# A two-block forward pass in fp32: the low parts of six of 434 chunks of weights are computed by GpSimd in place of VectorE

## The chip, the core and the metric

The kernel runs on one NeuronCore of one Trainium2 chip, as one program. The metric is the device time of one execution, in microseconds (us). Before the change it is 2494.46 us, the median of three runs between 2493.82 and 2494.64. The engines are named TensorE (PE in the rows), VectorE (DVE), ScalarE (ACT), GpSimd (POOL) and SyncE (SP).

## The reference, cut to what matters

256 tokens of width 2048 go through two blocks, each a mixer and an MLP around a residual stream. All is fp32, and nearly all of the time goes to products with weights.

```python
def first_block(x, ...):                     # one layer
    h = x + gla_mixer(rmsnorm(x, gla_norm), gla_w_in, ..., gla_w_out)
    h = h + sq_relu_mlp(rmsnorm(h, mlp_norm), mlp_w_up, mlp_w_down)
    return rmsnorm(h, final_norm)

def hybrid_mixer(xn, w_in, ...):             # the second block's mixer
    proj = xn @ w_in
    dn_qkv, dn_z, dn_a, dn_b, swa_q, swa_kv, sb_qkv, gates = split_cols(proj, IN_SIZES)
    dn_qkv = silu(causal_dwconv(dn_qkv, dn_conv))
    q, k, v = split_cols(dn_qkv, ...)        # 8 heads of 128
    q, k = l2norm(q), l2norm(k)
    o_dn = gated_delta_rule(q, k, v, g, beta)   # chunks of tokens; a triangular solve in each
    ...
    return merged @ w_o

def second_block(x, mem, ...):
    h = x + hybrid_mixer(rmsnorm(x, norm_mix), ...)
    h = h + memory_cross_attention(rmsnorm(h, norm_xattn), rmsnorm(mem, norm_mem), ...)
    h = h + conv_ffn(rmsnorm(h, norm_ffn), w_up, ffn_conv, w_down)
    return rmsnorm(h, norm_final)
```

The part that the change touches is `xn @ w_in` of the second block (its columns for queries, keys, values and z of the delta rule) and, beside it, the norms of q and k and the solve of the delta rule.

## The kernel before, in words

**Weights as a stream.** All weights lie in memory as 434 chunks of 128 x 2048 fp32 (1 MB), in the order in which they are used. TensorE takes them in a format of less precision (fp32r), so each chunk is split: ScalarE copies it, rounded, into `w_hi` (the high part, line 1044), and VectorE subtracts this from the raw chunk to get `w_lo` (the low part, line 1677). The activations are split likewise into `x_hi` and `x_lo`. A chunk is four tiles of 128 x 512; for each tile and each half of the tokens `chunk` (from line 508) issues three matmuls of 512 columns: high by high (L528), high by low (L529), low by high (L530). That makes 24 matmuls per chunk.

**Slots.** There are four slots. `w_raw` and `w_lo` share memory, so the subtraction works in place. SyncE loads chunk c when TensorE has finished chunk c - 4 (semaphore `used`). ScalarE and VectorE split the chunk that lies three ahead (`AHEAD = 3`) of the one for which they do their other work; their programs are written out by hand, step c of each holding the side work of chunk c and then `split(c + 3)`. TensorE waits ahead of chunk c for the semaphore `lo_ready` to have counted that far.

**The stretch.** The second block begins with chunk 192, and its chunks are counted here from there: chunk 18 is 192 + 18. Chunks 0 to 23 are queries, keys and values of the delta rule, 24 to 31 are z. Beside them, TensorE does side work between chunks, in this order from chunk 18 on:

- after 18: `nN` of the keys (products that turn them into rows, L693), then the products `kk` (L684); after 19: the products `qk` (L684); after 20: the transposes `dT` of the values (L548);
- after 24: `vN` of the first half of the values (L693) and the last `dT` (L548); after 26: the first products of the solve (L745); in the middle of 27: `vN` of the last half (L693), which waits for the semaphore `conv_out`, 6, that is for VectorE's `cv<-th,cv` (L1974) of step 25.

**VectorE's side work.** Step 19: the sum of squares `ssk` of the keys (L1978, L1983), `qkT`, `xT_c`, `xn_c`. Step 20: three taps of the convolution (L1965) and the scales from `rk`. Step 21: `cv<-th,cv` (L1974) and the opening of the solve, `xn_c` (L2022, L2023), `xT_c` (L2026), `xTb_c` (L2027), `am_c` (L2044). Steps 22 and 23: `am_c` and splits. Step 25: L1974 again.

**GpSimd** does small work: powers of minus one half for the norms (L461, L481, L483, L488), a memset of `xT` (L479), and issues some DMAs. `rk`, the inverse norms of the keys, is such a power of `ssk` (128x16, semaphore `ss_ready`, 2).

Of the kernel before, what the change touches and what calls it, by code (L numbers as in the profile page):

```python
# [16 lines left out]
def build(nc, x, x_turned, mem, mem_turned, stream, cols, rows, wglow, wab, wgu, shapes, masks, out):  # L17
# [14 lines left out]
    F32, F32R, BF16 = mybir.dt.float32, mybir.dt.float32r, mybir.dt.bfloat16  # L32
    ACT, ALU, AX = mybir.ActivationFunctionType, mybir.AluOpType, mybir.AxisListType
    N = 512
    NB = D // N
    SLOTS = 4
    AHEAD = 3
    EARLY = 4
    NCHUNK = stream.shape[0]
# [4 lines left out]
    with ExitStack() as ctx:  # L44
        def sem(name):
            return ctx.enter_context(nc.semaphore(name))
# [9 lines left out]
        def sb(name, shape, dt=F32, offset=None):  # L56
            nbytes = (2 if dt == BF16 else 4) * int(np.prod(shape[1:]))
            return nc.alloc_sbuf_tensor_at(name, shape, dt, offset=take(nbytes) if offset is None else offset)
# [4 lines left out]
        w_raw = sb("w_raw", [P, SLOTS, CH], F32, a_raw)  # L63
        w_lo = sb("w_lo", [P, SLOTS, CH], F32R, a_raw)
        w_hi = sb("w_hi", [P, SLOTS, CH], F32R)
# [158 lines left out]
        hi_ready, lo_ready, used = sem("hi_ready"), sem("lo_ready"), sem("used")  # L224
        tp_done = sem("tp_done")
        took = {k: {e: [sem(f"{k}_took_{e}{p}") for p in range(2)] for e in ("act", "dve")} for k in ("acc", "tp")}
        cols_in, cst_in, mask_in, gla_in, row_in, out_done = [sem(s) for s in ("cols_in", "cst_in", "mask_in", "gla_in", "row_in", "out_done")]
        x_in = sem("x_in")
        w_part = [[sem(f"w_part{c}_{k}") for k in range(4)] for c in range(EARLY)]
        gain_in, xT_in, x0_high, x0_low = sem("gain_in"), [sem(f"xT_in{n}") for n in range(NB + 1)], sem("x0_high"), sem("x0_low")  # L230
# [88 lines left out]
        ROUNDED = {name: k for k, name in enumerate(name for name in SIDE if name not in ("sbq", "sbk", "xk"))}  # L319
        LAST = {("norm1", 3): 1, ("merged", 3): 2, ("norm6", 3): 3}  # L320

        def ready(c, k=3):
            return 4 * c + k + 1 if c < EARLY else 3 * EARLY + c + 1

        def landing(c):
            return 16 * (c // SLOTS + (1 if c % SLOTS >= EARLY else 0))
# [71 lines left out]
        C_GLA, C_OUT, C_MLP, C_2 = 0, 48, 64, 192  # L398
# [47 lines left out]
        @block.gpsimd  # L446
        def _(pool):
            pool.memset(mhalf[:], -0.5).then_inc(pool_set, 1)
            pool.memset(glow[:], 0.0).then_inc(pool_set, 1)
            pool.wait_ge(w_part[2][3], 16)  # L450
            pool.dma_start(col[:, 16:N_COLS], cols[:, 16:N_COLS]).then_inc(cols_in, 16)
            pool.dma_start(wg_raw[:], wglow).then_inc(wg_in, 16)
            for r in range(4):
                pool.dma_start(w_gu[32 * r:32 * r + 16], wgu).then_inc(gla_in, 16)
            pool.dma_start(onorm[:], rows[:, 0:N]).then_inc(gla_in, 16)
            pool.wait_ge(pool_set, 1)
            mh8 = mhalf[:].rearrange("p (m h) -> p m h", m=M)

            def norm(j, count, k=0):
                pool.wait_ge(var_ready[k], count)  # L460
                pool.tensor_tensor(rstd[:, j], var[k][:], mhalf[:, 0:M], ALU.pow).then_inc(rstd_ready[k], 1)  # L461

            norm(0, 1)
            for hd in range(4):
                pool.wait_ge(ovar_s, hd + 1)
                pool.tensor_tensor(orstd[:, hd], ovar[:, hd], mhalf[:, 0:M], ALU.pow).then_inc(orstd_s, 1)

            pool.wait_ge(b_turned, SIDE["y", 3] + 1)
            pool.dma_start(frow[:], rows[:, N:N + D]).then_inc(row_in, 16)
            pool.dma_start(tri_c[:], shapes[:, 3 * P + SEQ:4 * P + SEQ]).then_inc(dn_in, 16)  # L470
            pool.dma_start(wab_raw[:], wab).then_inc(dn_in, 16)
            pool.dma_start(tri[:], shapes[:, 2 * P + SEQ:3 * P + SEQ]).then_inc(smalls_in, 16)
            pool.dma_start(lvl[:], masks[:, 0:6 * 32]).then_inc(smalls_in, 16)
            pool.dma_start(row_p[:], rows[:, N + 2 * D:]).then_inc(smalls_in, 16)
            norm(1, 2)

            norm(2, 3)
            norm(3, 4)
            pool.memset(xT[:], 0.0).then_inc(pool_set, 1)  # L479
            pool.wait_ge(ss_ready, 1)  # L480
            pool.tensor_tensor(rq[:], ssq[:], mh8, ALU.pow).then_inc(r_pow, 1)  # L481
            pool.wait_ge(ss_ready, 2)
            pool.tensor_tensor(rk[:], ssk[:], mh8, ALU.pow).then_inc(r_pow, 1)  # L483

            pool.wait_ge(tp_done, tps.name["up"] + 1)
            pool.dma_start(amask[:], masks[:, 6 * 32:]).then_inc(amask_in, 16)
            pool.wait_ge(y_var, 1)
            pool.tensor_tensor(yrs[:], yss[:], mh8, ALU.pow).then_inc(y_pow, 1)  # L488

            pool.wait_ge(used, C_WO)  # L490
            pool.dma_start(m_raw[:], mem_turned).then_inc(memT_in, 16)
            pool.wait_ge(b_low, ROUNDED["merged", 3] + 1)
            pool.dma_start(memt[:], mem.rearrange("(m p) n -> p m n", p=P)).then_inc(mem_in, 16)
            norm(4, 1, 1)
            norm(5, 5)

            pool.wait_ge(sq_done[1], 8)
            pool.dma_start(cw_all[:], cols[:, N_COLS:]).then_inc(cw_in, 16)
            norm(6, 6)
            pool.dma_start(frow2[:], rows[:, N + D:N + 2 * D]).then_inc(row2_in, 16)  # L500
            for m in range(M):
                pool.wait_ge(fin_var, m + 1)
                pool.tensor_tensor(rstd[:, 7, m:m + 1], var[1][:, m:m + 1], mhalf[:, 0:1], ALU.pow).then_inc(fin_rstd, 1)
# [3 lines left out]
        def _(pe):  # L507
            def chunk(c, lhs, k0, blk, first, last, n_k=4, width=N, rows_=(0, 1), done=True, second_half=None):

                if c >= EARLY:  # L510
                    pe.wait_ge(lo_ready, ready(c))
                if first and blk >= 2:

                    accs.wait(pe, blk - 2)
                wh = w_hi[:, c % SLOTS].rearrange("p (k n) -> p k n", n=width)
                wl = w_lo[:, c % SLOTS].rearrange("p (k n) -> p k n", n=width)
                for k in range(n_k):
                    if second_half and k == n_k // 2:
                        second_half()
                    if c < EARLY:  # L520
                        pe.wait_ge(lo_ready, ready(c, k))
                    if c < NB:
                        pe.wait_ge(x0_low, 4 * c + k + 1)
                    for m in rows_:
                        xh = lhs[0][:, k0 + k, m * P:(m + 1) * P]
                        xl = lhs[1][:, k0 + k, m * P:(m + 1) * P]
                        dst = acc[:, blk % 2, m, 0:width]
                        pe.matmul(dst, xh, wh[:, k], start=first and k == 0, stop=False)  # L528
                        pe.matmul(dst, xh, wl[:, k], start=False, stop=False)  # L529
                        mm = pe.matmul(dst, xl, wh[:, k], start=False, stop=last and k == n_k - 1)  # L530
                if done:
                    mm.then_inc(used, 1)
                return mm
# [108 lines left out]
            for c in range(48):  # L642
                b, q = divmod(c, 4)
                chunk(C_GLA + c, X, 4 * q, accs.name[("gla", b)], q == 0, q == 3)
                if c == 3:
                    pe.wait_ge(wg_l, 1)
                    sixteen_columns("glow_rows", wg)
                if c == 6:
                    pe.wait_ge(cst_in, 16)
                    sixteen_rows_back("glow", "glow_rows", glow_rows)  # L650
                if c == 8:
                    low_rank_transposed()
                if c == 10:
                    gate_logits()
                gla_side(c)

            for c in range(16):
                b, q = LATER(4)[c]
                if b == 0:
                    pe.wait_ge(b_low, ROUNDED["y", q] + 1)  # L660
                chunk(C_OUT + c, A, 4 * q, accs.name[("glaout", b)], q == 0, q == 3)
                gla_side(48 + c)
# [264 lines left out]
            for nb in range(NB):  # L927
                for j in range(16):
                    c = 50 + 16 * nb + j
# [734 lines left out]
        def _(dve):  # L1664
# [7 lines left out]

            def split(c):

                if c < NCHUNK:
                    dve.wait_ge(hi_ready, ready(c))
                    dve.tensor_tensor(w_lo[:, c % SLOTS], w_raw[:, c % SLOTS], w_hi[:, c % SLOTS].bitcast(F32),  # L1677
                                      ALU.subtract).then_inc(lo_ready, 1)
# [161 lines left out]
            for c in range(64):  # L1840
# [41 lines left out]
                if c and c not in (8, 10, 20, 24):  # L1882
                    split(c + AHEAD)
# [333 lines left out]
            for nb in range(NB):  # L2217
                for j in range(16):
                    c = 50 + 16 * nb + j
# [305 lines left out]
```

## Time and profile before

| what | value |
|---|---|
| median of the runs | 2494.46 us |
| the profiled execution, its time | 2494.04 us |
| its span, first to last instruction | 2492.2 us |
| mean granted TensorE clock (share of full) | 0.999 |
| TensorE busy | 2481.5 us, 100% |
| VectorE busy | 1490.1 us, 60% |
| ScalarE busy | 1541.5 us, 62% |
| GpSimd busy | 33.4 us, 1% |
| low parts on VectorE (L1677) | 430 of them, 983.6 us |

Busy time of TensorE is counted from the start of a matmul to its modelled end, and matmuls overlap, so 100% doesn't mean its peak. Idle time of the other engines costs nothing by itself. Times of rows are from the span's start.

### The profile page before, as it was taken

Reading aid. Unit: us, or ns where it says so; the run is one execution under the profiler, and the core shown is the slowest. Engines: PE = TensorE matmul, PEld = TensorE weight load, DVE = VectorE, ACT = ScalarE, POOL = GpSimd, SP = SyncE. Lnnn points to the kernel's source line nnn. Section 1 sums busy time; section 2 is a strip of 40 time slices with the busy share of each in tenths; the row PEclk is TensorE's granted clock in tenths of the full one; section 3 lists DMA queues with packets and bytes.
Section 4 is the critical chain, followed back from the end, with each engine's and each line's share of the span. In section 5 each row is a group of like instructions: output and inputs, shape, how many; then the busy total and the mean of one; then the engine's idle time right before and its main releaser. Section 6 shows DMA issues by size and latency. Waiting matters only on the chain.

```text
span 2492.2 us, 29745 instructions
## 1 busy us (share of the span) xinstructions
PE 2481.5 (100%) x12494; PEld 2051.3 (82%) x12494; DVE 1490.1 (60%) x1223; ACT 1541.5 (62%) x2041; POOL 33.4 (1%) x41
## 2 busy tenths in 40 slices
PE   9999999999999999999999999999999999999998
PEld 7887788888888888888888888888888888888887
DVE  5775656545545545666765665545565677646675
ACT  6645777636537547766465565535587688638873
POOL 0000000000000000000000000000000000000000
PEclk9999999999999999999999999999999999999999
DMA  8554555555555555545444445555655555555554
GB/s 287 187 200 163 187 200 187 199 188 196 192 193 196 190 199 187 201 169 187 154 160 145 155 162 193 193 196 189 267 188 185 186 188 199 187 198 191 195 193 152
DMA packets 69366, 472.37 MB, mean 190 GB/s; under 512 B 7912, under 2 KB 8352, under 8 KB 13424
## 3 DMA queue, kind: packets, MB, share of 16 engines
q1 hardware_dynamic: 67040, 460.62, 51.6%
q0 software_dynamic: 1312, 7.73, 0.8%
q8 instruction: 98, 1.61, 0.3%
q10 hardware_dynamic: 880, 2.11, 0.2%
q14 instruction: 36, 0.29, 0.0%
HBM read 468.33 MB, written 2.11 MB: 189 GB/s over the span
## 4 chain that ended last, share of the span: by engine, by line
PE 98%; DVE 1%; ACT 1%; issue 1%; DMA 0%; SPq 0%; POOLq 0%; POOL 0%; DVEq 0%; ACTq 0%
PE acc L528 31%; PE acc L530 31%; PE acc L529 31%; PE tp L812 1%; PE tp L548 0%; PE tp L745 0%; DMA x_raw<-in_x_turned 0%; PE tp L684 0%; PE tp L693 0%; DVE cv L1965 0%; DVE w_lo L1677 0%; PE tp L563 0%; PE tp L564 0%; PE tp L612 0%; PE tp L960 0%
## 5 line engine op out<-in xcount | busy, mean ns | idle before, releaser
L1677 DVE TENSOR_TENSOR w_lo<-w_raw,w_hi 128x2048 fp32r<-128x2048 f32 x430 | 983.6, 2289 | 730.9 <-ACT w_hi L1044 729.0
L1044 ACT ACTIVATE w_hi<-w_raw 128x2048 fp32r<-128x2048 f32 x430 | 823.0, 1916 | 482.4 <-DMA w_raw<-in_stream 462.3
L528 PE MATMUL acc<-w_hi,x_hi 128*128 128x512 f32 (+1 forms) x2240 | 875.1, 391 | 0.7 <-DVE w_lo L1684 0.4
L530 PE MATMUL acc<-w_hi,x_lo 128*128 128x512 f32 (+1 forms) x2240 | 868.4, 388 | 0.0
L529 PE MATMUL acc<-w_lo,x_hi 128*128 128x512 f32 (+1 forms) x2240 | 868.3, 388 | 0.0
L528 PEld LDWEIGHTS acc<-w_hi,x_hi 128*128 128x128 f32 x2240 | 420.6, 188 | 89.6 <-issue 2.0
L530 PEld LDWEIGHTS acc<-w_hi,x_lo 128*128 128x128 f32 x2240 | 420.6, 188 | 86.6
L529 PEld LDWEIGHTS acc<-w_lo,x_hi 128*128 128x128 f32 x2240 | 420.7, 188 | 85.5 <-issue 1.0
L528 PE MATMUL acc<-w_hi,a_hi 128*128 128x512 f32 x1120 | 436.3, 390 | 0.1
L530 PE MATMUL acc<-w_hi,a_lo 128*128 128x512 f32 x1120 | 435.7, 389 | 0.0
L529 PE MATMUL acc<-w_lo,a_hi 128*128 128x512 f32 x1120 | 435.7, 389 | 0.0
L528 PEld LDWEIGHTS acc<-w_hi,a_hi 128*128 128x128 f32 x1120 | 210.2, 188 | 43.9 <-DVE a_lo L2314 0.5
L530 PEld LDWEIGHTS acc<-w_hi,a_lo 128*128 128x128 f32 x1120 | 210.2, 188 | 43.7
L529 PEld LDWEIGHTS acc<-w_lo,a_hi 128*128 128x128 f32 x1120 | 210.2, 188 | 43.5
L1061 ACT ACTIVATE nat<-acc,rstd 128x512 f32<-128x512 f32 (+1 forms) x96 | 60.2, 679 | 115.2 <-PE acc L530 114.8
L1590 ACT ACTIVATE fm<-fturned 32x256 f32<-32x256 f32 x256 | 106.2, 415 | 4.2 <-DVE fturned L2355 1.2
L1244 ACT ACTIVATE sq<-turned 32x256 f32<-32x256 f32 x256 | 106.0, 414 | 3.0
L1753 DVE TENSOR_TENSOR h<-acc,h 128x1024 f32<-128x1024 f32 x35 | 42.8, 1223 | 43.9 <-PE acc L530 43.9
L1061 ACT ACTIVATE nat<-acc,rhalf 128x512 f32<-128x512 f32 x36 | 22.8, 686 | 72.2 <-PE acc L530 72.2
L1083 ACT ACTIVATE sq<-turned 32x256 f32<-32x256 f32 x104 | 43.2, 416 | 11.7 <-DVE turned L1720 10.5
L528 PE MATMUL acc<-w_hi,m_hi 128*128 128x512 f32 x128 | 49.8, 389 | 0.0
L529 PE MATMUL acc<-w_lo,m_hi 128*128 128x512 f32 x128 | 49.8, 389 | 0.0
(383 smaller groups left out, 1301.3 us busy)
## 6 DMA issues: line engine op xcount, KB each, us to landing
w_raw<-in_stream SPq DMA_DIRECT2D x430, 1024.0 KB, 4.8
w_raw<-in_stream SPq DMA_DIRECT2D x16, 256.0 KB, 8.1
h<-in_x SPq DMA_DIRECT2D x4, 512.0 KB, 14.0
frow<-in_rows POOLq DMA_DIRECT2D x2, 1024.0 KB, 6.2
m_raw<-in_mem_turned POOLq DMA_DIRECT2D x1, 2048.0 KB, 10.2
memt<-in_mem POOLq DMA_DIRECT2D x1, 2048.0 KB, 8.9
x_raw<-in_x_turned SPq DMA_DIRECT2D x3, 512.0 KB, 8.3
dec<-gc_rows ACTq DMA_DIRECT2D x1, 1024.0 KB, 6.1
```

What stands on the lines that cost most here:

```text
L528: pe.matmul(dst, xh, wh[:, k], start=first and k == 0, stop=False)
L529: pe.matmul(dst, xh, wl[:, k], start=False, stop=False)
L530: mm = pe.matmul(dst, xl, wh[:, k], start=False, stop=last and k == n_k - 1)
L812: mm = pe.matmul(tpf(g)[:, hd * P:(hd + 1) * P], lhs(hd), rhs(hd), start=True, stop=True)
L1044: act.activation(w_hi[:, c % SLOTS], w_raw[:, c % SLOTS], ACT.Copy).then_inc(hi_ready, 1)
L1061: ins = act.activation(dst[:, m], src[:, m], func, scale=scales[:, j, m:m + 1])
L1083: ins = act.activation(dst[32 * to:32 * to + 32, :, :, q], src[32 * q:32 * q + 32, :, :, to], ACT.Copy)
L1244: ins = act.activation(dst[32 * to:32 * to + 32, :, :, q], src[32 * q:32 * q + 32, :, :, to], ACT.Square)
L1590: ins = act.activation(dst[32 * to:32 * to + 32, :, :, q], src[32 * q:32 * q + 32, :, :, to], ACT.Copy)
L1677: dve.tensor_tensor(w_lo[:, c % SLOTS], w_raw[:, c % SLOTS], w_hi[:, c % SLOTS].bitcast(F32), ALU.subtract).then_inc(lo_ready, 1)
L1753: dve.tensor_tensor(hn, acc[:, blk % 2], hn, ALU.add).then_inc(accs.sem(blk), 1)
```

## The change

A list `POOLED` names six chunks, 18, 20, 22, 24, 26 and 28 of the second block. VectorE's `split` leaves them out. GpSimd's program gets a `split` of its own, with the same subtraction, which waits for the same high part and counts a semaphore of its own, `lo_pooled`. TensorE waits for `lo_pooled` ahead of a pooled chunk, and for `lo_ready`, less the pooled chunks so far, ahead of any other. GpSimd executes its row in order: the subtraction of chunk 18 stands between the powers for `rq` and `rk`, that of chunk 20 behind the power for `rk`.

```diff
+        POOLED = [192 + c for c in range(18, 30, 2)]
+
         def ready(c, k=3):
             return 4 * c + k + 1 if c < EARLY else 3 * EARLY + c + 1
+
+        def low_ready(eng, c):
+            if c in POOLED:
+                eng.wait_ge(lo_pooled, POOLED.index(c) + 1)
+            else:
+                eng.wait_ge(lo_ready, ready(c) - sum(1 for p in POOLED if p < c))
...
             pool.wait_ge(ss_ready, 1)
             pool.tensor_tensor(rq[:], ssq[:], mh8, ALU.pow).then_inc(r_pow, 1)
-            pool.wait_ge(ss_ready, 2)
-            pool.tensor_tensor(rk[:], ssk[:], mh8, ALU.pow).then_inc(r_pow, 1)
+            def split(c):
+                pool.wait_ge(hi_ready, ready(c))
+                pool.tensor_tensor(w_lo[:, c % SLOTS], w_raw[:, c % SLOTS], w_hi[:, c % SLOTS].bitcast(F32), ALU.subtract).then_inc(lo_pooled, 1)
+
+            for c in POOLED:
+                if c == C_2 + 20:
+                    pool.wait_ge(ss_ready, 2)
+                    pool.tensor_tensor(rk[:], ssk[:], mh8, ALU.pow).then_inc(r_pow, 1)
+                split(c)
...
                 if c >= EARLY:
-                    pe.wait_ge(lo_ready, ready(c))
+                    low_ready(pe, c)
...
             def split(c):
 
-                if c < NCHUNK:
+                if c < NCHUNK and c not in POOLED:
                     dve.wait_ge(hi_ready, ready(c))
```

Below, each row is one instruction: its line, its operation, out<-in by the program's names, the shape, and the semaphores it waits for. GpSimd's row around the powers, before:

```order
L479 MEMSET xT 128x2048
L481 TENSOR_TENSOR rq<-ssq,mhalf 128x16 [waits ss_ready]
L483 TENSOR_TENSOR rk<-ssk,mhalf 128x16 [waits ss_ready]
L486 DMA amask<-in_masks 128x768 [waits tp_done]
L488 TENSOR_TENSOR yrs<-yss,mhalf 128x16 [waits y_var]
```

and with the change (lines are those of the changed kernel, 8 to 15 further down):

```order
L487 MEMSET xT 128x2048
L489 TENSOR_TENSOR rq<-ssq,mhalf 128x16 [waits ss_ready]
L492 TENSOR_TENSOR w_lo<-w_raw,w_hi 128x2048 [waits hi_ready]
L497 TENSOR_TENSOR rk<-ssk,mhalf 128x16 [waits ss_ready]
L492 TENSOR_TENSOR w_lo<-w_raw,w_hi 128x2048 [waits hi_ready] x5
L501 DMA amask<-in_masks 128x768 [waits tp_done]
L503 TENSOR_TENSOR yrs<-yss,mhalf 128x16 [waits y_var]
```

One subtraction (chunk 18) stands ahead of the power for `rk`, five behind it, of which the first is chunk 20's.

VectorE's row from the low part of chunk 23 on (its first row here), before; the second low part is chunk 24's, the two in one row those of 25 and 26:

```order
L1677 TENSOR_TENSOR w_lo<-w_raw,w_hi 128x2048 [waits hi_ready,dve_step]
L1974 SCALAR_TENSOR_TENSOR cv<-th,cv 128x1024 [waits conv_t]
L2022 TENSOR_TENSOR xn_c<-xn_c,b_123 128x512
L2023 TENSOR_TENSOR xn_c<-lvl,xn_c 128x512 [waits dve_step]
L2026 STREAM_TRANSPOSE xT_c<-xn_c 128x512 [waits x_first]
L2027 TENSOR_TENSOR xTb_c<-xT_c,b_123 128x512 [waits dve_step]
L2044 TENSOR_TENSOR am_c_151<-aT_c,lvl 128x512 [waits dve_step]
L1677 TENSOR_TENSOR w_lo<-w_raw,w_hi 128x2048 [waits hi_ready]
L2044 TENSOR_TENSOR am_c_150<-aT_c,lvl 128x512
L1677 TENSOR_TENSOR w_lo<-w_raw,w_hi 128x2048 [waits hi_ready] x2
L1965 SCALAR_TENSOR_TENSOR cv<-tp,col,cv 128x255 [waits conv0]
```

and with the change:

```order
L1692 TENSOR_TENSOR w_lo<-w_raw,w_hi 128x2048 [waits hi_ready,dve_step]
L1989 SCALAR_TENSOR_TENSOR cv<-th,cv 128x1024 [waits conv_t]
L2037 TENSOR_TENSOR xn_c<-xn_c,b_123 128x512
L2038 TENSOR_TENSOR xn_c<-lvl,xn_c 128x512 [waits dve_step]
L2041 STREAM_TRANSPOSE xT_c<-xn_c 128x512 [waits x_first]
L2042 TENSOR_TENSOR xTb_c<-xT_c,b_123 128x512 [waits dve_step]
L2059 TENSOR_TENSOR am_c_151<-aT_c,lvl 128x512 [waits dve_step]
L2059 TENSOR_TENSOR am_c_150<-aT_c,lvl 128x512
L1692 TENSOR_TENSOR w_lo<-w_raw,w_hi 128x2048 [waits hi_ready]
L1980 SCALAR_TENSOR_TENSOR cv<-tp,col,cv 128x255 [waits conv0]
```

The low parts of 24 and 26 are gone, that of 25 stands directly behind the two `am_c`. Nothing else in VectorE's row changes place.

## Rows read from the trace of the kernel before

**Rows 1.** The page, busy times and costliest groups: busy us, mean ns, idle before.

```profile
PE 2481.5 (100%) x12494; PEld 2051.3 (82%) x12494; DVE 1490.1 (60%) x1223; ACT 1541.5 (62%) x2041; POOL 33.4 (1%) x41
...
L1677 DVE TENSOR_TENSOR w_lo<-w_raw,w_hi 128x2048 fp32r<-128x2048 f32 x430 | 983.6, 2289 | 730.9 <-ACT w_hi L1044 729.0
```

**Rows 2.** Timeline, TensorE: start us, us, instruction, count, idle before and its releaser.

```profile
1.19 6.15 PE L641 MATMUL acc<-junk 128*128 128x512 bf16 x16 [1.19 <-DVE junk L1807]
6.99 0.58 PE L528 MATMUL acc<-w_hi,x_hi 128*128 128x512 f32 x1
...
1188.36 0.39 PE L528 MATMUL acc<-w_hi,x_hi 128*128 128x512 f32 x1
...
1204.36 3.73 PE L684 MATMUL tp<-cqT,ckT 128*128 128x128 f32 x32
1207.84 0.48 PE L528 MATMUL acc<-w_hi,x_hi 128*128 128x512 f32 x1
...
1230.14 0.39 PE L529 MATMUL acc<-w_lo,x_hi 128*128 128x512 f32 x1
1230.37 0.39 PE L530 MATMUL acc<-w_hi,x_lo 128*128 128x512 f32 x1
1231.05 0.50 PE L528 MATMUL acc<-w_hi,x_hi 128*128 128x512 f32 x1 [0.30 <-DVE w_lo L1677]
...
1238.30 0.48 PE L528 MATMUL acc<-w_hi,x_hi 128*128 128x512 f32 x1
...
1253.45 1.03 PE L693 MATMUL tp<-consts,cv 128*128 128x128 f32 x8
...
2483.97 0.39 PE L530 MATMUL acc<-w_hi,a_lo 128*128 128x512 f32 x1
```

**Rows 3.** Timeline, GpSimd, from the memset to the power for rk.

```profile
1096.69 1.83 POOL L479 MEMSET xT<- 128x2048 f32 x1
1159.04 4.87 POOL L481 TENSOR_TENSOR rq<-ssq,mhalf 128x16 f32<-128x16 f32 x1 [60.52 <-DVE ssq L1983]
1204.12 2.90 POOL L483 TENSOR_TENSOR rk<-ssk,mhalf 128x16 f32<-128x16 f32 x1 [40.20 <-DVE ssk L1983]
```

**Rows 4.** Timeline, VectorE, around the same times and from step 19 to step 25.

```profile
1096.99 1.56 DVE L1699 TENSOR_SCALAR rhalf<-rstd 128x2 f32<-128x2 f32 x1
...
1158.87 2.29 DVE L1677 TENSOR_TENSOR w_lo<-w_raw,w_hi 128x2048 fp32r<-128x2048 f32 x1
...
1203.86 0.17 DVE L1983 TENSOR_SCALAR ssk<-ssk 128x16 f32<-128x16 f32 x1
...
1224.05 1.22 DVE L1974 SCALAR_TENSOR_TENSOR cv<-th,cv 128x1024 f32<-128x1024 f32 x1
1225.19 0.68 DVE L2022 TENSOR_TENSOR xn_c<-xn_c,b 128x512 f32<-128x512 f32 x1
...
1228.71 2.28 DVE L1677 TENSOR_TENSOR w_lo<-w_raw,w_hi 128x2048 fp32r<-128x2048 f32 x1
...
1231.52 2.28 DVE L1677 TENSOR_TENSOR w_lo<-w_raw,w_hi 128x2048 fp32r<-128x2048 f32 x1
...
1248.53 1.22 DVE L1974 SCALAR_TENSOR_TENSOR cv<-th,cv 128x1024 f32<-128x1024 f32 x1
```

**Rows 5.** Timeline, ScalarE, the high parts of chunks 18, 24 and 26.

```profile
1178.00 1.92 ACT L1044 ACTIVATE w_hi<-w_raw 128x2048 fp32r<-128x2048 f32 x1
...
1222.14 1.90 ACT L1044 ACTIVATE w_hi<-w_raw 128x2048 fp32r<-128x2048 f32 x1
...
1232.01 1.92 ACT L1044 ACTIVATE w_hi<-w_raw 128x2048 fp32r<-128x2048 f32 x1
```

**Rows 6.** Tile rhalf: duration ns min/median/max, first and last start us.

```profile
L1699 DVE TENSOR_SCALAR rhalf<-rstd x6: 169/169/1560, 52.4 to 1978.9; 128x2 f32<-128x2 f32 x6
```

**Rows 7.** Windows at the end: busy PE, PEld, DVE, ACT, POOL, granted clock, DMA.

```profile
2487.00:2488.00 1.00, 0.00 (x0) 0.00 (x0) 0.97 (x3) 0.48 (x1) 0.00 (x0) 0.91 0.00 0
2488.00:2489.00 1.00, 0.00 (x0) 0.00 (x0) 0.00 (x0) 0.00 (x0) 0.00 (x0) 0.50 0.96 348
```

More of the change, by code:

```diff
@@ L226, in build @@
         took = {k: {e: [sem(f"{k}_took_{e}{p}") for p in range(2)] for e in ("act", "dve")} for k in ("acc", "tp")}
-        cols_in, cst_in, mask_in, gla_in, row_in, out_done = [sem(s) for s in ("cols_in", "cst_in", "mask_in", "gla_in", "row_in", "out_done")]
+        cols_in, cst_in, mask_in, gla_in, row_in, out_done, lo_pooled = [sem(s) for s in ("cols_in", "cst_in", "mask_in", "gla_in", "row_in", "out_done", "lo_pooled")]
         x_in = sem("x_in")
```

## The prediction

> **What bounds the kernel now.** I read the page first: busy times, then the costliest groups. TensorE is busy for the whole span and VectorE for 60% of it [rows 1], so an edit that takes work from VectorE pays only where TensorE waits for VectorE. Then I followed TensorE in order of time through the stretch, chunks 18 to 28 of the delta rule's part (counted from its first chunk, as below). Chunk 24 is the one place where it waits for a low part: the last matmul of chunk 23 starts at 1230.37, 0.23 us behind the one before, and chunk 24 starts at 1231.05, at the end of VectorE's low part, not at 1230.60 [rows 2]. That is 0.45 us, all that six relieved chunks can give. A pitch of 0.227 us also makes a chunk's 24 matmuls 5.4 us. Next I read when each pooled chunk's high part is ready, when TensorE wants the chunk, and what GpSimd has ahead of it.
>
> **What goes, what comes.** VectorE loses six subtractions of 2.29 us [rows 1], 13.7 us of busy time. All but the last 0.45 us lies beside TensorE's work. GpSimd gains six subtractions of the same shape, in one row with its two powers, and the order shows the point on which the sum rests: the power for rk stands ahead of the low part of chunk 20 and waits for VectorE's sum ssk. Before, no chunk depended on that.
>
> **The duration of a GpSimd subtraction, X.** No row shows one. Below lies VectorE's own 2.29 us [rows 1], or still lower GpSimd's memset of the same 128x2048 at 1.83 us, which only writes [rows 3]. 1.83 us for 2048 elements is about 0.85 us per thousand for one stream after 0.1 us of start. Two reads in turn with the write beside them would take 3.6 us, two reads and the write all in turn 5.3 us. I take 4.4, the middle of these two, and keep 2.3 and 5.3 as ends. A far end is the power, 2.90 us for 16 elements [rows 3], which would make 0.37 ms of one chunk; the memset shows that moving an element doesn't cost that, and I give it no chance of weight. The Trainium skill, GPSIMD Engine Reference, section Elementwise — side-by-side cycle accounting, states 4497 ns for a two-input fp32 operation of 2048 elements; by it the sum below would be 4.1 in place of 3.9 us, and no run here shows it yet.
>
> **Chunk 18.** Its high part ends at 1178.00 + 1.92 = 1179.9 [rows 5], GpSimd is idle, and TensorE wants it at 1188.36 [rows 2]: 8.4 us of room. Cost nothing up to X = 8.4.
>
> **Chunk 20, the main term.** ssk ends at 1203.86 + 0.17 = 1204.03 [rows 4]. It isn't earlier for the two subtractions that VectorE no longer does, since products of TensorE and squares of ScalarE come before it. The power runs from 1204.12 to 1207.02 [rows 3], and the subtraction can only start then: it ends at 1207.02 + 4.4 = 1211.42. A semaphore takes 0.06 us to TensorE (1228.71 + 2.28 = 1230.99, and chunk 24 starts at 1231.05) [rows 2, 4]. So chunk 20 starts at 1211.48 in place of 1207.84 [rows 2]: a stall of **3.64 us**, called S = X - 0.76. Behind it on TensorE everything is queued, and nothing of it is won back, for TensorE has no other idle time. Chunk 22 is two chunks (10.9 us) later and GpSimd free at 1211.4, so its subtraction hides.
>
> **Chunk 24, the gain.** From here all times are of the profile before, with S to be added. High part 24 is ready at 1222.14 + 1.90 = 1224.04 [rows 5] and VectorE's low part 23 ends where cv starts, 1224.05 [rows 4]. GpSimd starts then, or behind the cv (1.2 us), and ends at 1228.5 to 1229.7, before 1230.60. The 0.45 us goes: **-0.45**.
>
> **The shared read.** Does GpSimd's subtraction hold up VectorE? The trace shows both directions. The power for rq starts at 1159.04 while VectorE's subtraction runs from 1158.87 to 1161.16, and takes 4.87 us; the same power for rk, with no such neighbour, takes 2.90 [rows 3, 4]. 1161.16 + 2.75 is its end: it stood still until VectorE had done. And a scaling of two elements on VectorE, 0.17 us in all other places, takes 1.56 us at 1096.99, until GpSimd's memset (1096.69 to 1098.52) ends [rows 3, 4, 6]. So I take it that VectorE's operations with two SBUF inputs and GpSimd's subtractions exclude each other for their whole length. The Trainium skill, SBUF — State Buffer, section Who interferes with whom, states this as an exclusive lock, taken by whoever issues first, for two-input VectorE operations against GpSimd's reads: by that rule, the trace agrees with its 4.87 against 2.90 us. Without such a lock the sum would be 3.64 - 0.45 = 3.2 us, and the first rival below would not exist.
>
> **Who is held up.** (a) Chunk 28: low part 27 ends on VectorE at about 1248.53, where cv starts [rows 4]; GpSimd, waiting, gets its turn and holds it until 1252.93. The cv on th (1.2 us) ends at 1254.13 in place of 1249.75, and TensorE wants it in the middle of chunk 27, at 1253.45 (L693) [rows 2, 4]: a stall of 1254.13 + 0.06 - 1253.45 = **0.74 us**, the cover of 3.7 us being gone. It is nothing for X under 3.6. (b) Chunk 25: the chain xn_c to am_c starts on VectorE when both GpSimd's low part 24 and cv are through, 1224.1 + 4.4 + 1.15 = 1229.65 in place of 1225.19, 4.46 us late. Low part 25 stood at 1231.52; less the 2.2 us of low part 24 and plus 4.46 it starts at 1233.8 [rows 4]. GpSimd asks for chunk 26 when the high part is through, 1232.01 + 1.92 = 1233.93 [rows 5], and 0.09 later as after ssk: 1234.0. VectorE is first by 0.2 us, and its low part 25 is ready at 1236.1, before the 1237.85 at which it is wanted (1238.30 less the 0.45). GpSimd then works on 26 until 1240.5, wanted at 1243.3. No cost, but by 0.2 us only.
>
> **Sum.** 3.64 - 0.45 + 0.74 = 3.93 us on the profiled execution, 2494.04 us (span 2492.2). The median of the runs stands 0.42 us above it, 2494.46, and gets the same shift: **2498.4 us**, +0.16%. A measurement of this kernel tells about 0.2% (5.0 us) from no change, so this is one that would hardly be told.
>
> **Rivals.**
> 1. GpSimd takes its turn for chunk 26 ahead of VectorE's low part 25 (the slower side). It decides from X = 4.6, or 0.2 us of lost time at the hand-overs. Then GpSimd runs 1234.0 to 1238.4, low part 25 ends at 1240.7, and chunk 25, wanted at 1237.85, stalls 2.89 us; the 0.74 of chunk 27 is covered by it. 3.64 - 0.45 + 2.89 = 6.1 us: 2500.5; at X = 5.3 it is 4.54 - 0.45 + 3.79 = 7.9: 2502.3. For it: the margin is thin. Against: at 4.4 the order comes out the other way. 27%.
> 2. The stall costs the clock too. TensorE idles from the end of the products at 1204.36 + 3.73 = 1208.09 to 1211.48, 3.4 us; nowhere else does it idle so long but at the end, where its last matmul ends at 2484.36 and the granted clock is 0.91 in 2487 to 2488, and 0.50 after, which puts its fall to the lower level, 1.2 GHz, at about 2487.8, 3.5 us later [rows 2, 7]. Price: at the opening 16 matmuls of 512 columns take 5.80 us in place of 16 x 0.227 = 3.6 [rows 2, 7], so +2.2: 2500.6. 9%.
> 3. GpSimd is quicker than I take it, or excludes nothing: X = 2.3 gives 1.54 - 0.45 = 1.1 us (2495.6), X = 3.6 gives 2.4 (2496.9), no lock 3.2. 16%.
> 4. No late chunk 20 at all, the gain alone: -0.45, 2494.0. It needs X under 0.76 us, less than half of the memset. 2%, and a gain over 0.2% is nowhere to be had.
> 5. The change does something else than it says: the order shows six subtractions in GpSimd's row and six gone from VectorE's, and TensorE waits for them. 1% at most, in the rest.
>
> **Chances and range.** The forecast has 42%, its own range 2497.6 to 2499.2. The rest, 4%, is a heavier mixture, rivals 1 and 2 together. The cases from 2495.6 to 2502.0 leave out less than 2 in 10 and take in X from 2.3 to about 5.2. Slower by over 0.2% (above 2499.45) are rivals 1 and 2, the heavier mixture, and a sliver of the forecast: 41%. Faster by over 0.2%: 1%. The rest, 58%, within.
>
> **What would show it.** GpSimd's row at 1207.0 gives X, and TensorE's wait of about 3.6 us ahead of chunk 20, released by GpSimd, is the main term. Chunk 24 should start without a wait. The cv on th ahead of the middle of chunk 27 should be drawn out and TensorE wait 0.8 us for it. If TensorE waits nearly 3 us at chunk 25, rival 1 holds; matmuls at twice the pitch behind chunk 20's wait are rival 2. Wrong outright would be: no wait at chunk 20, so that the power for rk came earlier, or a long wait at chunk 18 or 22.

## The result, and the profile after

The changed kernel takes 2500.38 us, the median of 15 runs (2498.22 to 2501.90), against 2494.58 us of 15 runs before (2493.82 to 2496.05). The ratio is 1.0022, with a 95% interval of 1.0014 to 1.0030: slower by 5.8 us. The time is inside the range on record, 2 us above the forecast, and above the 2499.45 us that the prediction set as the border of slower by over 0.2%, the side to which it gave 41%. The changed kernel's runs also lie further apart, 3.7 us against 2.2.

The page of the changed kernel, busy times and the group of VectorE's low parts, which answer to [rows 1]; lines of the code are 8 to 15 further down now:

```profile
PE 2482.4 (99%) x12494; PEld 2052.3 (82%) x12494; DVE 1487.1 (60%) x1217; ACT 1540.9 (62%) x2041; POOL 64.4 (3%) x47
...
L1692 DVE TENSOR_TENSOR w_lo<-w_raw,w_hi 128x2048 fp32r<-128x2048 f32 x424 | 969.9, 2289 | 731.0 <-ACT w_hi L1059 728.8
```

VectorE has given up 13.7 us in this group but only 3 us of its busy time: other operations of it have grown longer. The view of waits, TensorE alone (us in total, times, longest), shows what is new:

```profile
PE acc L543 <- POOL w_lo L492: 3.5, 1, 3.5
PE acc L543 <- DVE w_lo L1699: 2.2, 3, 0.9
...
PE tp L708 <- DVE cv L1989: 0.6, 1, 0.6
```

The first is the wait for GpSimd at chunk 20, the last the one in the middle of chunk 27. The second lies in the opening, ahead of the change, where the first weights landed later in this execution. Everything behind it stands later: GpSimd's first power by 0.64 us (52.32 against 51.68), the products ahead of chunk 20 by 1.13 (1205.49 against 1204.36). The other 0.5 us came up before 220 us, ahead of the change too; its cause isn't known. GpSimd's timeline, which answers to [rows 3]:

```profile
1181.13 4.59 POOL L492 TENSOR_TENSOR w_lo<-w_raw,w_hi 128x2048 fp32r<-128x2048 f32 x1 [16.09 <-ACT w_hi L1059]
1205.26 2.90 POOL L497 TENSOR_TENSOR rk<-ssk,mhalf 128x16 f32<-128x16 f32 x1 [19.53 <-DVE ssk L1998]
1208.12 9.49 POOL L492 TENSOR_TENSOR w_lo<-w_raw,w_hi 128x2048 fp32r<-128x2048 f32 x2
1230.40 5.62 POOL L492 TENSOR_TENSOR w_lo<-w_raw,w_hi 128x2048 fp32r<-128x2048 f32 x1 [12.79 <-ACT w_hi L1059]
1240.21 6.54 POOL L492 TENSOR_TENSOR w_lo<-w_raw,w_hi 128x2048 fp32r<-128x2048 f32 x1 [4.19 <-ACT w_hi L1059]
1253.88 4.80 POOL L492 TENSOR_TENSOR w_lo<-w_raw,w_hi 128x2048 fp32r<-128x2048 f32 x1 [7.13 <-ACT w_hi L1059]
```

The low part of chunk 20 begins at the end of the power, as forecast. The spans of 5.62 and 6.54 us are subtractions that stand still first, until VectorE's operation of that moment is done. TensorE's timeline, answering to [rows 2]:

```profile
1205.49 3.73 PE L699 MATMUL tp<-cqT,ckT 128*128 128x128 f32 x32
1212.68 0.80 PE L543 MATMUL acc<-w_hi,x_hi 128*128 128x512 f32 x1 [3.46 <-POOL w_lo L492]
1213.28 0.63 PE L544 MATMUL acc<-w_lo,x_hi 128*128 128x512 f32 x1
...
1214.98 0.63 PE L545 MATMUL acc<-w_hi,x_lo 128*128 128x512 f32 x1
1215.41 0.47 PE L543 MATMUL acc<-w_hi,x_hi 128*128 128x512 f32 x1
...
1236.58 0.39 PE L545 MATMUL acc<-w_hi,x_lo 128*128 128x512 f32 x1
1236.81 0.39 PE L543 MATMUL acc<-w_hi,x_hi 128*128 128x512 f32 x1
...
1243.91 0.48 PE L543 MATMUL acc<-w_hi,x_hi 128*128 128x512 f32 x1
...
1259.82 1.09 PE L708 MATMUL tp<-consts,cv 128*128 128x128 f32 x8 [0.60 <-DVE cv L1989]
```

Chunk 20 starts at 1212.68, 7.19 us behind the start of the products before it, in place of 3.48. The second matmul starts 0.60 us behind the first; from there to the seventh they are 0.43 us apart and last 0.63, where the later ones are 0.23 apart and last 0.39. Chunk 24 (1236.81) follows chunk 23 without a gap. The windows of this stretch (busy PE, PEld, DVE, ACT, POOL, granted clock, DMA) say what the wide spacing is:

```profile
1211.00:1212.00 1.00, 0.00 (x0) 0.00 (x0) 1.00 (x1) 0.00 (x0) 1.00 (x1) 1.00 0.00 0
1212.00:1213.00 1.00, 0.32 (x1) 0.32 (x2) 1.00 (x1) 0.00 (x0) 1.00 (x2) 0.58 0.00 0
1213.00:1214.00 1.00, 1.00 (x3) 0.81 (x3) 0.89 (x2) 0.00 (x0) 1.00 (x1) 0.50 0.00 0
...
1215.00:1216.00 1.00, 1.00 (x5) 0.81 (x4) 0.00 (x0) 0.00 (x0) 1.00 (x1) 0.72 0.00 0
```

The granted clock fell to 1.2 GHz (0.50) while TensorE waited and came back at about 1215.6. VectorE's timeline, answering to [rows 4]:

```profile
1209.26 1.23 DVE L1946 TENSOR_TENSOR qkT<-tp,dec 128x1024 f32<-128x1024 f32 x1 [0.56 <-PE tp L699]
1210.52 2.65 DVE L2026 TENSOR_TENSOR xT_c<-aT_c,lvl 128x512 f32<-128x512 f32 x1
...
1230.33 1.22 DVE L1989 SCALAR_TENSOR_TENSOR cv<-th,cv 128x1024 f32<-128x1024 f32 x1
1231.47 5.11 DVE L2037 TENSOR_TENSOR xn_c<-xn_c,b 128x512 f32<-128x512 f32 x1
...
1240.02 2.28 DVE L1692 TENSOR_TENSOR w_lo<-w_raw,w_hi 128x2048 fp32r<-128x2048 f32 x1
...
1254.15 5.61 DVE L1989 SCALAR_TENSOR_TENSOR cv<-th,cv 128x1024 f32<-128x1024 f32 x1
```

Three operations with two SBUF inputs that took 0.7 to 1.2 us before take 2.65, 5.11 and 5.61 us: each ends where GpSimd's subtraction has ended and its own time has passed, within 0.15 us (GpSimd ends at 1236.02 and `xn_c`, 0.68 us alone, at 1236.58). `qkT`, with one input in PSUM, keeps its 1.23 us beside the same subtraction. At 1240.02 the low part of chunk 25 begins, 0.19 us ahead of GpSimd's request at 1240.21.

The parts, from these rows against [rows 2] (differences of starts, so the 1.13 us from ahead of the change drop out):

| part | forecast | in the profiled execution |
|---|---|---|
| chunk 20 late: 7.19 - 3.48 | +3.64 | +3.71 |
| clock, and the wait at chunk 24: (1243.91 - 1212.68) - (1238.30 - 1207.84) | -0.45 | +0.77 |
| middle of chunk 27: (1259.82 - 1243.91) - (1253.45 - 1238.30) | +0.74 | +0.76 |
| sum | +3.93 | +5.24 |

The span grew by 6.5 us: these 5.24, the 1.13 from ahead of the change, and 0.1 elsewhere. The middle line is two things: the gain at chunk 24 and about 1.3 us of clock (the experiment with filled idling, below, gives -0.55 for the gain alone).

### The profile page after: what moved, and what is told of

Same layout as the page of the kernel before. It is cut to its first block, busy times and chain, and to the rows that moved or that the text cites. A ratio compares the mean times of both kernels' runs of the same rounds, so it can differ in the third digit from the quotient of the medians.

```text
span 2498.7 us, 29745 instructions
## 1 busy us (share of the span) xinstructions
PE 2482.4 (99%) x12494; PEld 2052.3 (82%) x12494; DVE 1487.1 (60%) x1217; ACT 1540.9 (62%) x2041; POOL 64.4 (3%) x47
## 4 chain that ended last, share of the span: by engine, by line
PE 97%; DVE 1%; ACT 1%; issue 0%; POOL 0%; DMA 0%; SPq 0%; POOLq 0%; DVEq 0%; ACTq 0%
PE acc L543 31%; PE acc L544 31%; PE acc L545 31%; PE tp L827 1%; PE tp L563 0%; PE tp L760 0%; DMA x_raw<-in_x_turned 0%; PE tp L708 0%; DVE cv L1989 0%; DVE cv L1980 0%; DVE w_lo L1692 0%; POOL w_lo L492 0%; PE tp L578 0%; PE tp L579 0%; PE tp L627 0%
## 5 line engine op out<-in xcount | busy, mean ns | idle before, releaser
L1692 DVE TENSOR_TENSOR w_lo<-w_raw,w_hi 128x2048 fp32r<-128x2048 f32 x424 | 969.9, 2289 | 731.0 <-ACT w_hi L1059 728.8
```

## The experiments

Theory: the late power ahead of chunk 20 is the main term, a second one is VectorE held up by GpSimd's reads ahead of the middle of chunk 27, and the 2 us on top with the spread are the clock, which falls because TensorE idles. Rivals: contention makes the loss wherever the power stands; or the surplus comes from the turn for chunk 26, which the forecast had only 0.2 us from going wrong. All medians stand beside runs of the kernel before on the same chip: 2494.55 us for `rk_behind`, `only_20`, `idle_filled` and `rk_behind_no28`, 2494.46 for `half_20`, `am_twice` and `memset_28`.

**The power behind the low part of chunk 20** (`rk_behind`).

```diff
-                if c == C_2 + 20:
+                if c == C_2 + 22:
                     pool.wait_ge(ss_ready, 2)
                     pool.tensor_tensor(rk[:], ssk[:], mh8, ALU.pow).then_inc(r_pow, 1)
                 split(c)
```

> All six subtractions on GpSimd, but the power for rk stands behind the low part of chunk 20 in GpSimd's row. Theory (the late power is the main term, and the idle of TensorE it makes costs clock on top): no wait at chunk 20, granted clock full all through the stretch; the wait ahead of chunk 24 gone (-0.6 us), 0.8 us in the middle of chunk 27 stays: +0.2 us on before, 2494.8, runs as close together as before's. Rival (GpSimd's subtractions cost by holding up VectorE, wherever the power stands): still over +3 us.

Measured: 2494.79 us (2494.39 to 2495.73), ratio 1.0002 (0.9993 to 1.0011). TensorE's waits and GpSimd's timeline in it:

```profile
PE tp L708 <- DVE cv L1989: 0.6, 1, 0.6
PE acc L543 <- DVE w_lo L1699: 0.4, 1, 0.4
```

```profile
1193.01 4.77 POOL L492 TENSOR_TENSOR w_lo<-w_raw,w_hi 128x2048 fp32r<-128x2048 f32 x1 [8.18 <-ACT w_hi L1059]
1204.36 2.90 POOL L497 TENSOR_TENSOR rk<-ssk,mhalf 128x16 f32<-128x16 f32 x1 [6.58 <-DVE ssk L1998]
```

The low part of chunk 20 is through at 1197.78, 6.6 us before the power can start. The wait for GpSimd is gone, the one for cv is still there, and 5.6 of the 5.8 us have gone with one number in the code. All six subtractions still run on GpSimd, so contention wherever the power stands is not what makes the loss; what it costs is the wait of 0.6 us that is left.

**Chunk 20 alone** (`only_20`).

```diff
-        POOLED = [192 + c for c in range(18, 30, 2)]
+        POOLED = [212]
```

> Only chunk 20 is pooled, behind the power for rk. Theory: the wait of 3.7 us at chunk 20 and 0 to 3 us of lower clock behind it; chunk 24 waits for VectorE as before or a little less, nothing at chunk 27: +5 to +6 us in the median, 2500, with a spread over several us. Rival (the contention of the other five makes half of the loss): about +3.7 us and no spread.

Measured: 2499.58 us (2498.11 to 2501.16), ratio 1.0020 (1.0011 to 1.0029). TensorE's timeline and windows:

```profile
1204.69 3.73 PE L699 MATMUL tp<-cqT,ckT 128*128 128x128 f32 x32
1211.86 0.80 PE L543 MATMUL acc<-w_hi,x_hi 128*128 128x512 f32 x1 [3.44 <-POOL w_lo L492]
...
1217.58 0.51 PE L544 MATMUL acc<-w_lo,x_hi 128*128 128x512 f32 x1
...
1220.20 1.03 PE L563 MATMUL tp<-consts,nat 128*128 128x128 f32 x8
```

```profile
1210.00:1211.00 1.00, 0.00 (x0) 0.00 (x0) 1.00 (x1) 0.00 (x0) 1.00 (x1) 0.99 0.00 0
1211.00:1212.00 1.00, 0.14 (x1) 0.14 (x1) 1.00 (x1) 0.00 (x0) 0.81 (x1) 0.50 0.00 0
...
1217.00:1218.00 1.00, 1.00 (x4) 0.77 (x4) 0.00 (x0) 0.00 (x0) 0.00 (x0) 0.59 0.00 0
```

One chunk makes 5.0 of the 5.8 us and nearly the whole spread, a little below the 2500 expected. Three of the 11 runs are at 2498.11 to 2498.40, where the wait alone would put them (2494.55 + 3.7), the others at 2499.42 or above. Here the lower clock lasted from 1211.0 to 1217.8, and the chunk takes 8.34 us (1211.86 to 1220.20).

**The idling filled** (`idle_filled`).

```diff
+                if c == 212:
+                    accs.wait(pe, blk - 2)
+                    for _ in range(16):
+                        pe.matmul(acc[:, blk % 2, 0, :], junk[:, 0:P], junk[:], start=True, stop=True)
                 if c >= EARLY:
                     low_ready(pe, c)
```

> The changed kernel with 16 matmuls of 512 columns on scratch data ahead of TensorE's wait for chunk 20; they fill the 3.5 us of idling and compute nothing that is used. Theory (the clock falls because TensorE idles): chunk 20 starts at the same moment as in the changed kernel, but its matmuls are 0.23 us apart from the start: 2498.3 to 2498.6, +3.8 to +4.1 us on before, spread under 1 us. Rival (the 2 us above the forecast and the spread come from the turn for chunk 26, which TensorE would feel at chunk 25): 2500.4 and the spread of the changed kernel.

Measured: 2498.45 us (2498.14 to 2499.28), ratio 1.0016 (1.0007 to 1.0025). TensorE's timeline and one window (15 of the 16 matmuls on scratch data are in the trace):

```profile
1204.77 3.73 PE L703 MATMUL tp<-cqT,ckT 128*128 128x128 f32 x32
1208.55 3.40 PE L528 MATMUL acc<-junk 128*128 128x512 bf16 x15
1211.96 0.50 PE L547 MATMUL acc<-w_hi,x_hi 128*128 128x512 f32 x1
...
1217.55 1.03 PE L567 MATMUL tp<-consts,nat 128*128 128x128 f32 x8
...
1241.87 0.48 PE L547 MATMUL acc<-w_hi,x_hi 128*128 128x512 f32 x1
```

```profile
1212.00:1213.00 1.00, 1.00 (x5) 0.82 (x6) 0.96 (x2) 0.00 (x0) 1.00 (x1) 1.00 0.00 0
```

Chunk 20 starts 7.19 us behind the products, as in the changed kernel, but at the full clock: it takes 5.59 us (1211.96 to 1217.55) in place of 6.92 there. The median is 3.9 us above before, which is the forecast's sum, and the spread of 3.7 us has shrunk to 1.1. So the surplus over the forecast, 2500.38 - 2498.45 = 1.9 us in the median and 3.5 at most, is the clock, and it fell because TensorE idled: the two kernels differ only in the scratch matmuls. From chunk 20 to 25 it is 29.91 us against 30.46 before: the gain at chunk 24 is 0.55 us.

**Half of chunk 20** (`half_20`).

```diff
+                own = slice(CH // 2, CH) if c == 212 else slice(0, CH)
-                pool.tensor_tensor(w_lo[:, c % SLOTS], ...
+                pool.tensor_tensor(w_lo[:, c % SLOTS, own], ...
...
-                if c < NCHUNK and c not in POOLED:
+                if c < NCHUNK and (c not in POOLED or c == 212):
+                    own = slice(0, CH // 2) if c == 212 else slice(0, CH)
```

The cut also leaves out TensorE's side: ahead of chunk 20 it waits for both halves.

> The changed kernel, but of chunk 20 GpSimd takes only the second 1024 columns, behind the power for rk; VectorE takes the first 1024 in its old place. Theory (the wait is the rest of GpSimd's subtraction behind the power, and the clock falls only after a longer idling): the subtraction takes about 2.3 us in place of 4.5, TensorE waits 1.5 us at chunk 20, idles 1.3, the clock stays up: 1.5 - 0.6 + 0.8 = +1.7 us, 2496.3, no spread. Rival (any wait of that kind costs clock, or the duration of a GpSimd subtraction is mostly start-up): +3 us or more.

Measured: 2496.28 us (2495.95 to 2496.60), ratio 1.0007 (0.9998 to 1.0016). TensorE's timeline:

```profile
1204.63 3.73 PE L700 MATMUL tp<-cqT,ckT 128*128 128x128 f32 x32
1209.64 0.50 PE L544 MATMUL acc<-w_hi,x_hi 128*128 128x512 f32 x1 [1.28 <-POOL w_lo L493]
```

The wait follows the size of the subtraction (5.01 us behind the products, 1.53 more than before), and after 1.3 us of idling the clock is still full: chunk 20 takes 5.58 us (1209.64 to 1215.22), and the 11 runs lie within 0.7 us.

**One operation more ahead of the low part of chunk 25** (`am_twice`), on top of the moved power.

```diff
+                        if l == 2:
+                            link(dve.tensor_tensor(mat4(am_c[l % 2][:]), mat4(aT_c[:]), lvl[:, l + 1]..., ALU.mult))
                         dve.tensor_tensor(mat4(am_c[l % 2][:]), mat4(aT_c[:]), lvl[:, l + 1]..., ALU.mult).then_inc(m_ready, 1)
```

> The power for rk stands behind the low part of chunk 20, and VectorE does one of its am_c of step 22 twice (0.7 us more, ahead of the low part of chunk 25). Theory (turns at the shared read are taken in the order of asking, and VectorE had it for chunk 25 by 0.2 us only): GpSimd takes its turn for chunk 26 first, the low part of chunk 25 is 4.5 us late, TensorE waits about 3.6 us at chunk 25 and not at 27: +2.8 us on the kernel without the doubled operation, 2497.6, and up to 3 us more where the clock falls in that wait. Rival (GpSimd and VectorE only slow each other a little, and VectorE has 4 us of slack): 2494.8, no wait at chunk 25.

Measured: 2499.40 us (2497.43 to 2500.97), ratio 1.0020 (1.0011 to 1.0028). VectorE, GpSimd, TensorE, and two windows:

```profile
1234.47 0.69 DVE L2061 TENSOR_TENSOR am_c<-aT_c,lvl 128x512 f32<-128x512 f32 x1
1235.08 6.64 DVE L1692 TENSOR_TENSOR w_lo<-w_raw,w_hi 128x2048 fp32r<-128x2048 f32 x1
```

```profile
1234.56 5.01 POOL L492 TENSOR_TENSOR w_lo<-w_raw,w_hi 128x2048 fp32r<-128x2048 f32 x1 [4.20 <-ACT w_hi L1059]
```

```profile
1237.47 1.04 PE L563 MATMUL tp<-consts,nat 128*128 128x128 f32 x8
1241.77 0.79 PE L543 MATMUL acc<-w_hi,x_hi 128*128 128x512 f32 x1 [3.27 <-DVE w_lo L1692]
1242.36 0.63 PE L544 MATMUL acc<-w_lo,x_hi 128*128 128x512 f32 x1
```

```profile
1240.00:1241.00 1.00, 0.00 (x0) 0.00 (x0) 1.00 (x1) 1.00 (x2) 0.00 (x0) 0.97 0.85 360
1241.00:1242.00 1.00, 0.23 (x1) 0.23 (x2) 1.00 (x2) 0.99 (x1) 0.00 (x0) 0.50 0.01 0
```

GpSimd asked at 1234.56 and got its turn at about 1235.1, VectorE's subtraction of 2.3 us took 6.64, TensorE waited 3.3 us for it, and the clock fell again, at about 1240.9. This is the prediction's first rival, made to happen: 0.7 us of work on an engine with time to spare costs 4.7 us: 4.9 over its kernel before, where `rk_behind` stands 0.2 over its own. In the changed kernel's profile it didn't happen, and 1.1 us of spread in `idle_filled`, with the same order, leave no room for it in any of those runs.

**A write in place of the subtraction of chunk 28** (`memset_28`), with the moved power.

```diff
+                if c == 220:
+                    pool.memset(w_lo[:, c % SLOTS].bitcast(F32), 0.0).then_inc(lo_pooled, 1)
+                else:
```

> The power for rk stands behind the low part of chunk 20, and for chunk 28 GpSimd only writes zeros over the slot (128x2048) in place of subtracting, so this chunk's low part is left out of the computation. Theory (a two-input operation of VectorE is held up by GpSimd's reads, not by its writes): VectorE's cv on th beside it takes 1.2 us, as with an idle GpSimd, though the memset runs for 1.8 us at the same time; no wait at chunk 27. Rival (any GpSimd operation holds VectorE up): cv takes about 2.8 us.

Measured: 2494.44 us in a single run; the reading is from its trace. GpSimd and VectorE:

```profile
1248.47 1.81 POOL L493 MEMSET w_lo<- 128x2048 f32 x1 [7.11 <-ACT w_hi L1062]
```

```profile
1248.75 1.22 DVE L1992 SCALAR_TENSOR_TENSOR cv<-th,cv 128x1024 f32<-128x1024 f32 x1
```

cv keeps its 1.22 us beside the memset, where it took 5.61 beside the subtraction, and TensorE has no wait at chunk 27. It is GpSimd's reading that holds up an operation of two SBUF inputs. The Trainium skill, SBUF — State Buffer, section Who interferes with whom, says just this; the trace agrees with 1.22 against 5.61 us.

**Five chunks, the power moved** (`rk_behind_no28`).

```diff
-        POOLED = [192 + c for c in range(18, 30, 2)]
+        POOLED = [192 + c for c in range(18, 28, 2)]
```

and the power moved as in `rk_behind`.

> The power for rk behind the low part of chunk 20, and chunk 28 back on VectorE, so five are pooled. Theory: no wait at chunks 20, 24 and 27: -0.6 us on before, 2494.0, within what can be told from no change. Rival (the wait at chunk 27 comes from VectorE's later work, not from GpSimd's turn): 2494.8 as with all six.

Measured: 2493.93 us (2493.46 to 2495.27), ratio 0.9998 (0.9989 to 1.0007). No wait for cv is left. The median is 0.6 us below before's, as the gain at chunk 24 asks, but the interval holds no change.

## Why the prediction was right, and where it was off

- **Chunk 20, 3.64 us: right.** The order showed the power ahead of the subtraction, and the trace of before gave its end. Measured 3.71, and moving the power takes it away.
- **X, 4.4 us: right.** The changed kernel's shortest is 4.51 us. The Trainium skill's 4497 ns (GPSIMD Engine Reference, the side-by-side cycle accounting) is what this trace shows, and the middle of the two counts of streams was near it by luck as much as by reason: nothing in the trace of before says how reads and writes share the time.
- **The shared read: right, on one good row and one that shows something else.** The power for rq (4.87 us) was held up by a two-input subtraction. The scaling that took 1.56 us stood beside a memset, which only writes, and `memset_28` shows that a memset doesn't hold up a two-input operation. So that row is a hold-up of another kind, which no run here takes apart, and no evidence for this lock.
- **Chunk 24, -0.45: right**, -0.55 measured; the sum left out that behind the wait the matmuls didn't start at full pace: chunk 24 took 5.58 us in the profile of before (1231.05 to 1236.63) and 5.44 in the changed kernel's (1236.81 to 1242.25).
- **Middle of chunk 27, 0.74: right**, 0.76.
- **Chunk 25, 0.2 us of margin: right.** 0.19 in the profile. That the rival behind it was real is shown by `am_twice`.
- **The clock: wrong in its chance, near in its size by luck.** It stood as the second rival at +2.2 us with 9%. Without it the kernel takes 2498.45; of the changed kernel's 15 runs two (2498.22 and 2498.39) are at that level, the others 2499.85 or above. So, by the times (only one of the 15 has a trace), it happened in about 13 of 15. The runs' mean granted clocks agree as far as they tell: 0.998 in nine of the 13, 0.999 in all runs of `idle_filled` and in all those of the kernel before that stand beside the experiments.
- **The step that failed** is the reading of the end of the trace: there the clock fell 3.5 us after the last matmul, and I took 3.4 us of idling for a near miss. One event shows one delay. In the changed kernel it fell at about 1212.2, 2.9 us after the products ended (1209.22); in `only_20` at 1211.0, 2.6 us after (1208.42), in `am_twice` at 1240.9, 2.4 us after (1238.51). The ends of the nine traces spread further: the fall came 2.2 us after the last matmul in `half_20` and 4.8 in the changed kernel, whose last matmul ends at 2490.80:

```profile
2495.00:2496.00 1.00, 0.00 (x0) 0.00 (x0) 0.00 (x0) 0.00 (x0) 0.00 (x0) 0.78 1.01 367
```

- The price of 2.2 us came from the 16 matmuls of one opening. The same 16 take 6.15 us in the profile of before and 4.91 in the changed kernel's, so another execution would have given a price 1.2 us lower, and in both the granted clock of the windows there reads 1.00: that they ran at the lower level was taken from their pace alone. What the fall costs varies as much: chunk 20 takes 5.55 us in before, 6.92 in the changed kernel's profile, 8.34 in `only_20`'s.
- The forecast's own range, 2497.6 to 2499.2, missed therefore; the stated range held, since the clock was priced in it.

## What to carry to other kernels

An engine with 1% of busy time is not free at every moment: before work is moved into its queue, look up what stands ahead of it there and what that waits for. Where the bound engine then waits, count the wait and, for an idling of about 3.5 us, a clock penalty of 1 to 3.5 us, and take the fall as the usual case: by their times it came in about 31 of the 37 executions here that idled 3.3 to 3.5 us (the changed kernel, `only_20`, `am_twice`), and in none of the 11 of `half_20`, which idled 1.3. GpSimd's subtractions take turns with VectorE's operations on two SBUF inputs, in the order of asking, so here a margin of 0.2 us in who asks first was worth 3 us of waiting.

## What the runs showed of the hardware

- TensorE's clock at 1.2 GHz lasted about 3.4 us in the changed kernel's profile (1212.2 to 1215.6) and 6.8 us in `only_20` (1211.0 to 1217.8) and `am_twice` (1240.9 to 1247.8), after idling of nearly the same length (3.46, 3.44 and 3.27 us); TensorE took up work 0.5, 0.9 and 0.8 us after the fall. Whether it falls and how long it stays low spreads the time of one program over 3.5 us.
- A subtraction of GpSimd and an operation of VectorE that stand still for one another are recorded with their whole wait as busy time (6.54 for 4.5 us of work, 5.61 for 1.2). The busy time of VectorE fell by 3 us only, though 13.7 us of work had left it.
